# Attention of a hybrid decoder on one core: one maximum for both heads of a pair, one copy for both branches' turned weights

## What is computed

```
ss  = einsum('bqgrd,bgqkld->bgrqkl', qb, ks)            # branch b=0: selected blocks
p_s = masked_softmax(ss, m_s);   o_s = p_s @ vs
sw  = einsum('bqgrd,bgkd->bgrqk', qb, kw)               # branch b=1: window
o_w = masked_softmax(sw, m_w) @ vw
return gb[..., 0:1] * o_c + gb[..., 1:2] * o_s + gb[..., 2:3] * o_w
```

## Time and profile before

| | |
|---|---|
| median of 3 runs | 942.92 us (942.9 to 943.16) |
| profiled execution | 943.52 us, its span on the core 941.8 us |
| PE busy | 892.7 us, 95% of the span |
| DVE busy | 587.9 us, 62% |
| ACT busy | 523.2 us, 56% |
| attention over the head pairs | about 621 to 698 us of the span |
| granted TensorE clock | 1.0 over the span |

### The profile page before, as it was taken

How to read it: one execution, slowest core, us unless ns; L and a number is a source line. 1 busy time by engine, 2 the same in 40 slices (tenths; PEclk the granted TensorE clock), 3 DMA queues, 4 the chain that set the end, 5 groups by cost and what they waited for, 6 DMA issues and landing times.

```text
span 941.8 us, 14028 instructions
## 1 busy us (share of the span) xinstructions
PE 892.7 (95%) x5289; PEld 757.7 (80%) x5289; DVE 587.9 (62%) x980; ACT 523.2 (56%) x931; POOL 23.8 (3%) x46
## 2 busy tenths in 40 slices
PE   6989999999899999999999999999889999999998
PEld 5989978788788878888888788887567788888876
DVE  5876984858666575555544666767757555554465
ACT  6645756676767465444443558356866544443452
POOL 6000000000000000000000000000000000000000
PEclk9999999999999999999999999999999999999999
DMA  9941211111114547777546654420035556654552
GB/s 343 333 138 42 90 46 46 46 46 45 46 46 158 183 152 227 233 231 259 187 158 199 201 179 158 156 90 2 1 95 174 179 181 188 187 196 162 191 185 95
DMA packets 105898, 138.28 MB, mean 147 GB/s; under 512 B 4585, under 2 KB 76786, under 8 KB 105842
## 3 DMA queue, kind: packets, MB, share of 16 engines
q1 hardware_dynamic: 103650, 130.15, 42.8%
q0 software_dynamic: 2160, 7.36, 2.1%
q10 hardware_dynamic: 32, 0.01, 0.0%
HBM read 136.45 MB, written 1.05 MB: 146 GB/s over the span
## 4 chain that ended last, share of the span: by engine, by line
PE 73%; DVE 12%; ACT 11%; issue 2%; DMA 1%; SPq 0%; ACTq 0%; DVEq 0%
PE ps L504 17%; PE ps L506 16%; PE ps L505 16%; PE ps L483 4%; DVE w_lo L1586 4%; ACT w_hi L1114 4%; PE ps L488 3%; PE ps L489 3%; PE ps L490 3%; PE ps L735 3%; PE ps L717 2%; DVE gdn L1653 2%; PE ps L1000 1%; ACT qkvT L1520 1%; DVE gdn L1789 1%
## 5 line engine op out<-in xcount | busy, mean ns | idle before, releaser
L1586 DVE TENSOR_TENSOR w_lo<-w_raw,w_hi 128x2048 fp32r<-128x2048 f32 (+2 forms) x100 | 220.7, 2207 | 195.9 <-ACT w_hi L1114 195.8
L1114 ACT ACTIVATE w_hi<-w_raw 128x2048 fp32r<-128x2048 f32 (+2 forms) x100 | 184.5, 1845 | 182.0 <-PE ps L506 143.1
L504 PE MATMUL ps<-w_hi,x_hi 128*128 128x512 f32 x480 | 193.6, 403 | 11.2 <-DVE gdn L1820 5.7
L506 PE MATMUL ps<-w_hi,x_lo 128*128 128x512 f32 x480 | 187.5, 391 | 0.0
L505 PE MATMUL ps<-w_lo,x_hi 128*128 128x512 f32 x480 | 187.2, 390 | 0.0
L504 PEld LDWEIGHTS ps<-w_hi,x_hi 128*128 128x128 f32 x480 | 90.2, 188 | 34.2 <-DVE gdn L1820 7.5
L506 PEld LDWEIGHTS ps<-w_hi,x_lo 128*128 128x128 f32 x480 | 90.1, 188 | 19.5
L505 PEld LDWEIGHTS ps<-w_lo,x_hi 128*128 128x128 f32 x480 | 90.4, 188 | 16.5
L488 PE MATMUL ps<-x_hi,w_hi 128*128 128x256 f32 x320 | 91.5, 286 | 1.1 <-DVE w_lo L1586 0.8
L489 PE MATMUL ps<-x_lo,w_hi 128*128 128x256 f32 x320 | 90.6, 283 | 0.0
L490 PE MATMUL ps<-x_hi,w_lo 128*128 128x256 f32 x320 | 90.5, 283 | 0.0
(11 more groups left out here) (311 smaller groups left out, 1470.7 us busy)
## 6 DMA issues: line engine op xcount, KB each, us to landing
w_raw<-in_ffn_w_in SPq DMA_DIRECT2D x88, 512.0 KB, 4.6
w_raw<-in_ffn_w_out SPq DMA_DIRECT2D x40, 512.0 KB, 4.3
w_raw<-in_gdn_w_in SPq DMA_DIRECT2D x28, 512.0 KB, 4.7
gdn<-in_gdn_w_in SPq DMA_DIRECT2D x20, 512.0 KB, 7.4
w_raw<-in_gdn_w_out SPq DMA_DIRECT2D x16, 512.0 KB, 4.2
w_raw<-in_ple_w_gate SPq DMA_DIRECT2D x16, 512.0 KB, 4.6
w_raw<-in_kv_w SPq DMA_DIRECT2D x12, 512.0 KB, 4.1
qkvT<-in_cmp_w POOLq DMA_DIRECT2D x8, 512.0 KB, 5.0
```

Of the source, the lines that this page charges most:

```text
L504: mm(o, hi, w_h, start=first and kk == 0, stop=False, skip_group_check=True)
L506: return mm(o, lo, w_h, start=False, stop=end and kk == n - 1, skip_group_check=True)
L1114: A(whi[:, place(stage, q), c0:c0 + n], ring_raw(u) if stage == "qkv" else raw[:, q, 0:n], ACT.Copy).then_inc(S["hi_done"], 1)
L1586: V.tensor_tensor(wlo[:, s, c0:c0 + n], ring_raw(u) if stage == "qkv" else raw[:, q, 0:n], whi[:, s, c0:c0 + n], ALU.subtract).then_inc(S[ ...
```

## The change

Two kinds of instruction are merged, and the banks of the scores are laid out so that the first merge can be written as one access.

- `maxima(p, t)` reduces both heads at once: 128 partitions, 2 heads, 2 branches, 128 or 256 columns. It waits for both heads' last mask product. Two per pair instead of four.
- ACT's `turned(p, e)` copies both branches, banks 6 and 7, in one ACTIVATE of 128x768, after all six transposes. Two per pair instead of four. `pts_act` rises once per head.
- PE's `turned(p, e)` waits, for either branch, for that one copy of the head before.
- The scores of block 0 lie in banks 2 and 3 (heads 0 and 1), of block 1 in banks 4 and 5.

PE's list of instructions is the same, but for bank addresses and the values that it waits for. What was `mx..._dve` once per head is now once per pair and block; the exponentials of both heads wait for that one.

```
-                o = [bank(2 + 2 * e, 2, T) if t else bank(3 + 2 * e, 2, P) for e in range(2)]
+                o = [bank(4 + e, 2, T) if t else bank(2 + e, 2, P) for e in range(2)]
@@ PE turned(p, e)
                 for b in range(2):
                     pe.wait_ge(S["pw_dve"], 4 * p + 2 * e + b + 1)
                     if p or e:
-                        pe.wait_ge(S["pts_act"], 4 * p + 2 * e + b - 1)
+                        pe.wait_ge(S["pts_act"], 2 * p + e)
@@ PE output(p)
-                pe.wait_ge(S["pts_act"], 4 * p + 4)
+                pe.wait_ge(S["pts_act"], 2 * p + 2)
@@ PE, loop, p == 3
-                    pe.wait_ge(S["pts_act"], 16)
+                    pe.wait_ge(S["pts_act"], 8)
@@ ACT exps(p)
-                    i, s1, s0 = 2 * (p % 2) + e, bank(2 + 2 * e, 2, T), bank(3 + 2 * e, 2, P)
-                    act.wait_ge(S["mx0_dve"], 2 * p + e + 1)
+                    i, s1, s0 = 2 * (p % 2) + e, bank(4 + e, 2, T), bank(2 + e, 2, P)
+                    act.wait_ge(S["mx0_dve"], p + 1)
...
-                    act.wait_ge(S["mx_dve"], 2 * p + e + 1)
+                    act.wait_ge(S["mx_dve"], p + 1)
@@ ACT turned(p, e)
-                for b in range(2):
-                    act.wait_ge(S["ptr_ps"], 4 * p + 2 * e + b + 1)
-                    A(pts[:, p % 2, e, b], bank(6 + b, 3, P), ACT.Copy).then_inc(S["pts_act"], 1)
+                act.wait_ge(S["ptr_ps"], 4 * p + 2 * e + 2)
+                A(pts[:, p % 2, e].rearrange("p b s q -> p b (s q)"), ps[:, 6:8, 0:3 * P], ACT.Copy).then_inc(S["pts_act"], 1)
@@ DVE
-            def maxima(p, e, t):
-                dve.wait_ge(S["sc_ps"], 4 * p + 2 * t + e + 1)
-                i, o = 2 * (p % 2) + e, bank(2 + 2 * e, 2, T) if t else bank(3 + 2 * e, 2, P)
-                V.tensor_reduce(out=hst[:, i, 1, 2 * t:2 * t + 2], in_=o, axis=AX, op=ALU.max,
+            def maxima(p, t):
+                dve.wait_ge(S["sc_ps"], 4 * p + 2 * t + 2)
+                i, n = 2 * (p % 2), T if t else P
+                o = ps[:, 2 + 2 * t:4 + 2 * t, 0:2 * n].rearrange("p e (b q) -> p e b q", b=2)
+                V.tensor_reduce(out=hst[:, i:i + 2, 1, 2 * t:2 * t + 2], in_=o, axis=AX, op=ALU.max,
                                 negate=True).then_inc(S["mx_dve" if t else "mx0_dve"], 1)
```

More of the change, by code:

```diff
@@ L2194, in _ @@
             for t in range(TT):
-                for e in range(2):
-                    maxima(0, e, t)
+                maxima(0, t)
             cmp_shifted(0, 6)
@@ L2201, in _ @@
             for t in range(TT):
-                for e in range(2):
-                    maxima(1, e, t)
+                maxima(1, t)
             cmp_weighted(0)
@@ L2208, in _ @@
                 if p < 7:
-                    maxima(p + 1, 0, 0)
-                    maxima(p + 1, 1, 0)
+                    maxima(p + 1, 0)
                 weights(p, 1)
                 if p < 7:
-                    maxima(p + 1, 0, 1)
-                    maxima(p + 1, 1, 1)
+                    maxima(p + 1, 1)
                 if p == 1:
```

## The result

| | before | changed |
|---|---|---|
| runs beside each other, first time | 943.37 us, median of 6 (942.9 to 943.85) | 947.04 us, median of 6 (945.19 to 949.5) |
| runs beside each other, second time | 944.44 us, median of 26 (942.91 to 945.55) | 947.06 us, median of 7 (945.18 to 948.25) |
| profiled execution | 943.52 us, span 941.8 | 946.99 us, span 945.2 |
| instructions of ACT and DVE in the profile | 931 and 980 | 915 and 964 |

The ratio to the kernel before was 1.0037 the first time, with a 95% interval of 1.0027 to 1.0047, and 1.0029 (1.0018 to 1.0040) the second. The change is slower, by 0.3 to 0.4%. The forecast had the sign, and had put the time 2 us too low: 947.04 lies above its range. The two kernels also scatter differently: 26 runs before span 2.6 us, six runs changed 4.3 us.

The account below looks back on a forecast made before the run. It took the attention loop's chain of waits between ACT and PE, 6.83 us a pair, as the bound. Terms 0.45 + 1.3 + 0.2 = +1.95 us on 942.92 gave 944.9 us, range 943.9 to 946.3.

Parts of the forecast that it names:

- pairs 2 to 6, each: Head 1's merged copy in the attention loop waits for the sixth transpose, delaying the next exponential: +0.26 us per pair.
- pair 0: Ahead of PE's query products, head 1's six transposes wait for head 0's merged copy and end later: +0.45 us.
- pair 7: Ahead of the wo products, PE's last six transposes start later behind head 0's merged copy: +0.2 us.
- copy of 768 columns: ACT's merged copy lands after 0.81 us and occupies ACT for 0.70 us before the next instruction.
- maximum of 1024 columns: DVE's merged block 1 reduction takes about 1225 ns, covered before head 0's exponential needs it: 0 us.
- banks: New PSUM banks for the scores cost 0 us; bounds 0.18 us a pair either way, 0.9 us over five.
- sum: Whole kernel: 0.45 + 1.3 + 0.2 = +1.95 us, expected to reach the end whole.
- 1.02 - 0.75: Head 1's copies, pairs 2 to 6: next exponential 1.02 us after the first copy's present start, instead of 0.75.
- Rival C: Merged instructions cost more at the bank's end: copy 0.98 us, 0.17 more in seven places, 946.2 us; chance 0.19.
- Rival B: Faster: 16 copies and 16 reductions fewer, each saving 0.06 us fixed time, 1.9 us in all, 941.0; chance 0.04.
- Late next: nothing that I can find: After head 0's copies in pairs 1 to 6, nothing else comes late; output and the exponentials move along together.
- Rival A: Much of the loss hidden by cover in pairs 0 and 7 or a later transfer wait: 944.0 us; chance 0.17.

Follow-up runs that it names:

- early_both_merged1: early_both_swap with head 1's copies of both branches merged into one; median 941.46 us, ratio 0.9972 to the kernel before.
- early_both_swap: Kernel before with both heads' next block 0 exponentials ahead of head 1's copies, and PE's next block 0 scores ahead of output from pair 3; 941.18 us, ratio 0.9976.
- merged_head0: Kernel before with only head 0's copies merged in each pair, head 1's left split; median 945.33 us, ratio 1.0013.
- merged_pair7: Kernel before with a single merged copy, that of head 0 in pair 7; median 945.09 us, ratio 1.0014.
- copies_only: Kernel before with the merged copies of both heads alone, banks and maxima as before; median 947.30 us, ratio 1.0032.

## Why the prediction was wrong, point by point

**Right: the chain and the place of the loss.** ACT and PE take turns in the loop, DVE is not on the chain; the merged copy gives up the overlap with the second three transposes.

**Right, nearly to size: the terms.**

| term | forecast | measured |
|---|---|---|
| pairs 2 to 6, each | +0.26 | +0.27 |
| pair 0 | +0.45 | +0.46 |
| pair 7 | +0.2 | +0.3 |
| copy of 768 columns | 0.81, next after 0.70 | 0.81, next after 0.70 |
| maximum of 1024 columns | 1.22, hidden | 1.22, hidden |
| banks | 0 | 0 (loop 67.39 against 67.36) |
| sum | +1.95 | +2.10 to +2.14 |

The forecast's own subtraction, 1.02 - 0.75, is 0.27 and not 0.26. In pairs 0 and 7 PE waited for the copy, as forecast, though the rows name DVE; it started 0.10 and 0.15 us behind the copy's end instead of 0.05, which is what pair 7 was short of. Rival C, a bank boundary that is paid, falls at 812 ns. Rival B's fixed part of 0.06 us is real, but it was got back only where the operand was already there and the copy on the chain, twice in early_both_merged1, 0.14 us together. The rule of the Trainium skill that was named beside the sum (Perfetto Trace Analysis, Optimizing Scalar/DVE Operations: breaking instructions up may help where an engine isn't saturated and holds others up) agrees with these runs: with merged copies the loop is 2.1 us longer than with split ones. The other rule of that section, that grouping can help if the engine is saturated, was not put to the test: even in early_both_swap ACT was busy 5.76 of the 6.24 us of a steady pair.

**Wrong: the step from the sum to the time.** The forecast added the sum to 942.92, said that the shift would reach the end whole, and closed the range 1.4 us above, at 946.3. It put two things at nothing.

First, the scatter of the base. Three runs within 0.26 us were taken for the kernel's time, though the profiled execution on the same record, 943.52, already lay above all three; 79 later runs went from 942.78 to 945.79, with medians of 943.6 to 944.4 in three sets. One cause is the transfer that ACT waits 1.7 us longer for in five of fourteen profiles. The profiled run of before had it early, that of the changed kernel late. Between these two the sum is closed: 943.52, and 1.5 before the loop, 2.14 in it and 0.25 less behind it, give 946.9, and 946.99 was measured. The median of 947.04 stands 0.05 us beside that run, at the same clock of 1.0, so that the late transfer is the likely reason why it lies above the range; no trace of that run was kept. Beside the runs of before of the same set (943.37) the loop's 2.1 us alone would give 945.5, inside the range. That most of the six changed runs were probably late ones, and the six beside them (942.9 to 943.85) probably not, is chance as far as the runs tell.

Second, the clock. The forecast took the granted clock of 1.0 as given. In five of 13 runs of the changed kernel it was not: 948.0 against 946.3 us, some 0.65 us on average over all, and 1.6 us where two profiles caught it. That belongs to the change, and it lifts the mean more than the median: only two of the six runs scored had it (947.78 and 949.5).

Inside the working, the paragraph on pair 7 is where the second was missed: it priced the later start of the last transposes at 0.2 us, and did not ask what the longer idle time ahead of `wo` might do to PE itself. "Late next: nothing that I can find", said of head 0's copies in pairs 1 to 6, held: merged_head0 lost nothing there. Rival A, that some of the loss would be hidden, took 0.17 of the chance with no row that spoke for it; no rival stood for a late transfer or a lower clock.

## What to carry to other kernels

Before merging two instructions, look at what each of them waits for. If the engine is idle ahead of the first, stands on the chain, and the second's operand comes later (here 0.32 us), the merge costs that interval less the fixed part (here 0.06 us), at each turn of the chain; if the operand is there when the engine arrives, it brings the fixed part back, and off the chain it does neither. The idle time itself is the thing to use: moving two exponentials into it was worth 0.3%, where merging lost 0.3%. When a row names what an engine waited for, check that the instruction needs it: here it named DVE where the copy came last. And a few runs that agree don't give the spread of a kernel; a range should hold what a late transfer can do.

## What the runs showed of the hardware

- One ACTIVATE may read across two PSUM banks at no extra cost: 812 ns for 768 columns in two banks, where 384 in one took 496. A TENSOR_REDUCE took 687 ns for 512 columns in two banks and 683 in one; 1024 columns in two banks took 1220 ns, where a TENSOR_TENSOR of 1024 columns from SBUF took 1225.
- The granted clock fell to 0.50 for about 3.4 us in the `wo` products (profiles of merged_pair7 and copies_only), after PE had been idle 0.65 us, busy 1.01 and idle 1.05. A mean clock of 0.998 or less came in 14 of 42 runs of the kernels with that gap of 1.05 us, in one of seven where it was filled, and in none of 147 where it was 0.60 or 0.32 (other orders of the loop among them). Single gaps of 1.06 to 1.47 us elsewhere in the same profiles had no such drop behind them.
- ACT waited 1.7 us longer for one of the 256 KB weight transfers of the first layer's input embedding in five profiles of fourteen, with the same program ahead of it.
